# Two more boundaries of a two-block model take the "ahead" form, and the ahead steps are regrouped

## The reference

```python
def modulate(z, g, shift, scale):
    return rmsnorm(z, g) * (1.0 + scale) + shift
def swiglu(h, wi, wo):
    a, u = jnp.split(h @ wi, 2, axis=-1)
    return (jax.nn.silu(a) * u) @ wo
# in each layer, three times with different parts:
x = x + 0.5 * m[2] * swiglu(modulate(x, norm_g[l, 0], m[0], m[1]), ffn1_wi[l], ffn1_wo[l])
```

## Time and profile before

| | us |
|---|---|
| median of three executions | 3223.28 |
| the profiled execution | 3223.28 |
| its span, first to last instruction | 3221.5 |
| matmul engine busy | 3134.3 (97%) |
| VectorE busy | 1885.6 (59%) |
| ScalarE busy | 1035.2 (32%) |

### The profile page before, as it was taken

How to read it: one execution, slowest core, us unless ns; L and a number is a source line. 1 busy time by engine, 2 the same in 40 slices (tenths; PEclk the granted TensorE clock), 3 DMA queues, 4 the chain that set the end, 5 groups by cost and what they waited for, 6 DMA issues and landing times.

```text
span 3221.5 us, 37195 instructions
## 1 busy us (share of the span) xinstructions
PE 3134.3 (97%) x15095; PEld 2518.2 (78%) x15106; DVE 1885.6 (59%) x2713; ACT 1035.2 (32%) x1498; POOL 10.2 (0%) x23
## 2 busy tenths in 40 slices
PE   8999999998899999999999999999999998899998
PEld 6888888776678888788877888788887764578887
DVE  7876555646575554666656554566665555574444
ACT  4212222335542222322234222332224444442222
POOL 0000000000000000000000000000000000000000
PEclk9999999999999999999999999999999999799999
DMA  6433332210034443255522443235552210133231
GB/s 230 140 118 129 146 124 85 65 45 11 1 138 138 149 144 118 91 203 189 204 86 79 175 139 131 79 118 204 188 183 63 72 53 1 53 118 104 93 98 52
DMA packets 102422, 367.13 MB, mean 114 GB/s; under 512 B 11311, under 2 KB 12607, under 8 KB 101997
## 3 DMA queue, kind: packets, MB, share of 16 engines
q1 hardware_dynamic: 101212, 360.04, 32.7%
q0 software_dynamic: 1040, 4.71, 0.4%
HBM read 362.61 MB, written 2.10 MB: 113 GB/s over the span
## 4 chain that ended last, share of the span: by engine, by line
PE 88%; DVE 6%; ACT 3%; issue 1%; DMA 1%; SPq 0%; POOL 0%; DVEq 0%; ACTq 0%; POOLq 0%
PE ps L192 25%; PE ps L194 25%; PE ps L193 25%; PE ps L196 4%; PE ps L197 2%; DVE SQ L614 1%; PE ps L499 1%; DVE HL L603 1%; PE ps L2888 1%; DVE WL L184 1%; PE ps L2858 1%; DVE XT L1037 0%; PE ps L2788 0%; PE ps L2555 0%; DVE RAW L1499 0%
## 5 line engine op out<-in xcount | busy, mean ns | idle before, releaser
L192 PE MATMUL ps<-HH,WH 128*128 128x512 f32 x2432 | 959.5, 395 | 6.9 <-DVE HL L603 3.1
L194 PE MATMUL ps<-HH,WL 128*128 128x512 f32 x2432 | 947.7, 390 | 0.0
L193 PE MATMUL ps<-HL,WH 128*128 128x512 f32 x2432 | 946.9, 389 | 0.0
L179 ACT ACTIVATE WH<-RAW 128x1024 fp32r<-128x1024 f32 x456 | 458.5, 1047 | 622.0 <-PE ps L194 367.2
L184 DVE TENSOR_TENSOR WL<-RAW,WH 128x1024 fp32r<-128x1024 f32 x456 | 542.9, 1220 | 78.0 <-ACT WH L179 77.8
L192 PEld LDWEIGHTS ps<-HH,WH 128*128 128x128 f32 x2432 | 456.5, 188 | 116.1 <-issue 12.2
L194 PEld LDWEIGHTS ps<-HH,WL 128*128 128x128 f32 x2432 | 456.5, 188 | 96.8
L193 PEld LDWEIGHTS ps<-HL,WH 128*128 128x128 f32 x2432 | 456.8, 188 | 95.9 <-issue 4.3
L1037 DVE SCALAR_TENSOR_TENSOR XT<-ps,DER,XT 128x512 f32<-128x512 f32 x512 | 346.6, 683 | 249.9 <-PE ps L194 235.1
L192 PE MATMUL ps<-GH,WH 128*128 128x512 f32 x1056 | 412.9, 391 | 4.8 <-DVE GL L945 4.8
L194 PE MATMUL ps<-GH,WL 128*128 128x512 f32 x1056 | 411.1, 389 | 0.0
(11 more groups left out here) (382 smaller groups left out, 2542.5 us busy)
## 6 DMA issues: line engine op xcount, KB each, us to landing
RAW<-in_w_modt SPq DMA_DIRECT2D x200, 512.0 KB, 5.0
RAW<-in_ffn_wi SPq DMA_DIRECT2D x178, 512.0 KB, 4.9
RAW<-in_w_gu SPq DMA_DIRECT2D x90, 512.0 KB, 4.5
RAW<-in_ffn_wo SPq DMA_DIRECT2D x88, 512.0 KB, 4.9
RAW<-in_w_in SPq DMA_DIRECT2D x44, 512.0 KB, 3.6
RAW<-in_w_down SPq DMA_DIRECT2D x44, 512.0 KB, 4.2
RAW<-in_w_out SPq DMA_DIRECT2D x16, 512.0 KB, 4.5
STG<-in_w_modt SPq DMA_DIRECT2D x10, 512.0 KB, 12.8
```

Source lines behind the costliest of these rows:

```text
L179: act.e.activation(u.hi, u.ld.view, ACT.Copy).then_inc(u.hi_done.sem, 1)
L192: pe.e.matmul(out, wh, x[0], start=first, stop=False)
L193: pe.e.matmul(out, wh, x[1], start=False, stop=False)
L194: m = pe.e.matmul(out, wl, x[0], start=False, stop=last)
```

## The change

* Stages 3 and 5 take the ahead form too: the last down of stage 2 and the pool mixer write UH and UL and full sums of squares; the bias dots for them run in the tails of stages 2 and 3; stages 3 and 5 begin with Factor, NormSplit and chunk 0 on UH and UL. The norm sums, spreads and fillers before these two stages and the filler Busy(4) of the pool mixer go.
* AheadHi and AheadLo become one step, AheadSplit, placed after the product step of d (before, AheadHi stood in front of it), and the last sum of squares, SumsEnd, stands after AheadSplit of block 6 instead of before AheadLo of block 6.
* UpRest goes; its work is part of Up for chunk 0, before the splits of chunk 2.
* Factor's matmul stands after k=2 instead of k=1, and Root after the square of block 6 instead of block 2.
* With the ahead form, the condition spread and the modulation dots of stages 3 and 5 start two chunks later.

```diff
             P.total = self.add[7]
         elif k == 7:
             P.sat = [(P.SA, self.add[5]), (P.SQ[:, 0, :], self.sq[6]), (P.SQ[:, 1, :], self.sq[7])]
-        if k == (2 if self.full else 6):
+        if k == 6:
             self.root = Root(P)
     def square(self, act, k):
...
         act.wait_ge(*self.gain)
         act.e.activation(P.UH[:, k, :], P.XT[:, k, 0:T], ACT.Identity, scale=P.mod_a(self.mi, k)).then_inc(self.hi.sem, 1)
-
-class AheadLo(Step):
-
-
-    def __init__(self, of):
-        self.of = of
-
-    def vector(self, dve):
-        of = self.of
-        P, k = of.P, of.k
-        dve.wait_ge(*of.hi)
-        dve.e.scalar_tensor_tensor(P.UL[:, k, :], P.XT[:, k, 0:T], P.mod_a(of.mi, k), P.UH[:, k, :].bitcast(F32),
-                                   ALU.mult, ALU.subtract).then_inc(of.lo.sem, 1)
+    def vector(self, dve):
+        P, k = self.P, self.k
+        dve.wait_ge(*self.hi)
+        dve.e.scalar_tensor_tensor(P.UL[:, k, :], P.XT[:, k, 0:T], P.mod_a(self.mi, k), P.UH[:, k, :].bitcast(F32),
+                                   ALU.mult, ALU.subtract).then_inc(self.lo.sem, 1)
 class Factor(Step):
...
                 for k in range(8):
                     for q in range(2):
                         products(q, n, k)
-                    if self.factor and k == 1:
+                    if self.factor and k == 2:
                         self.factor.sum(pe)
         else:
             for q in range(2):
...
                 act.wait_ge(*self.done[q, n])
                 if q == 0:
                     act.wait_ge(*self.sfree[n])
+                if q == 0 and self.factor:
+                    act.wait_ge(*self.scaled[q])
+                    act.wait_ge(*self.biased)
+                    act.e.activation(s, s, ACT.Silu, bias=P.BIAS[:, q:q + 1]).then_inc(self.silu[n].sem, 1)
+                    continue
                 if n:
                     if q:
                         act.wait_ge(*self.sxfree)
...
                     dve.wait_ge(*self.factor.done)
                     dve.wait_ge(*self.sfree[n])
                     dve.e.tensor_tensor(d, out, self.factor.R, ALU.mult).then_inc(self.scaled[q].sem, 1)
+                    if q:
+                        dve.wait_ge(*self.silu[n])
+                        dve.wait_ge(*self.scaled[q])
+                        dve.wait_ge(*self.biased)
+                        dve.e.scalar_tensor_tensor(s, d, P.BIAS[:, q:q + 1], s, ALU.add, ALU.mult).then_inc(self.mul[n].sem, 1)
+                        dve.wait_ge(*self.hi[n])
+                        dve.e.tensor_tensor(gl, s, gh.bitcast(F32), ALU.subtract).then_inc(self.lo[n].sem, 1)
                     continue
                 if n:
                     d = F.SX[:, :] if q else s
...
                     dve.e.tensor_tensor(s, s, F.SX[:, :] if n else out, ALU.mult).then_inc(self.mul[n].sem, 1)
                     dve.wait_ge(*self.hi[n])
                     dve.e.tensor_tensor(gl, s, gh.bitcast(F32), ALU.subtract).then_inc(self.lo[n].sem, 1)
-
-
-class UpRest(Step):
-
-
-
-    def __init__(self, up):
-        self.up = up
-
-    def scalar(self, act):
-        up = self.up
-        F, P = up.F, up.P
-        s, gh, gl = up.tiles(0)
-        act.wait_ge(*up.scaled[0])
-        act.wait_ge(*up.biased)
-        act.e.activation(s, s, ACT.Silu, bias=P.BIAS[:, 0:1]).then_inc(up.silu[0].sem, 1)
-        act.wait_ge(*up.mul[0])
-        act.wait_ge(*F.gfree.get(up.c - F.NG, NONE))
-        act.e.activation(gh, s, ACT.Copy).then_inc(up.hi[0].sem, 1)
-
-    def vector(self, dve):
-        up = self.up
-        F, P = up.F, up.P
-        s, gh, gl = up.tiles(0)
-        dve.wait_ge(*up.silu[0])
-        dve.wait_ge(*up.scaled[1])
-        dve.wait_ge(*up.biased)
-        dve.e.scalar_tensor_tensor(s, F.S[:, 1, :], P.BIAS[:, 1:2], s, ALU.add, ALU.mult).then_inc(up.mul[0].sem, 1)
-        dve.wait_ge(*up.hi[0])
-        dve.e.tensor_tensor(gl, s, gh.bitcast(F32), ALU.subtract).then_inc(up.lo[0].sem, 1)
 class Down:
...
                     if dot and fs == tail[0]:
                         bias["lds"] = self.bias_loads(dot[1])
                     for d in range(8):
-                        if nxt is not None and last and d:
-                            hi = self.add(AheadHi(self, nxt, d - 1, down.evac[d - 1, 0][0]))
                         self.add(DownPart(down, d))
                         if nxt is not None and last and d:
-                            if d == 7:
-                                self.add(SumsEnd(sums))
-                            self.add(AheadLo(hi))
+                            self.add(AheadSplit(self, nxt, d - 1, down.evac[d - 1, 0][0]))
                         if d in (1, 3, 5):
                             split_ahead()
                         if dot and fs == tail[0] and d == 5:
...
                         if dot and fs == tail[1] and d in (2, 4):
                             self.add((BiasSum if d == 2 else BiasCopy)(bias["dot"]))
                     if nxt is not None and last:
-                        self.add(AheadLo(self.add(AheadHi(self, nxt, 7, down.evac[7, 0][0]))))
+                        self.add(SumsEnd(sums))
+                        self.add(AheadSplit(self, nxt, 7, down.evac[7, 0][0]))
                 return ([wo[f] for f in fs], run, "in pieces")
             tail, jobs, halves, first = groups[-2:], [], [], 2 if ahead else 0
...
         def job(d):
             def run(units):
-                hi = self.add(AheadHi(self, nxt, d - 1, evac[d - 1])) if d else None
                 out = self.add(OutMM(self, mi, mix, d, units[0], bfree, sums))
                 self.over, evac[d] = out.done, out.evac
-                if d == 7:
-                    self.add(SumsEnd(sums))
                 if d:
-                    self.add(AheadLo(hi))
+                    self.add(AheadSplit(self, nxt, d - 1, evac[d - 1]))
                 if d == 1:
                     bias["lds"] = self.bias_loads(wi)
                 elif d == 2:
...
                 means[g] = self.add(PoolMean(self, copies[g], M, band, ztile, bfree))
             def add(g):
-                return [self.add(PoolAdd(self, mi, means[g], o, bfree, sums)) for o in range(2)][1]
+                for o in range(2):
+                    k = 2 * g + o
+                    adds[k] = self.add(PoolAdd(self, mi, means[g], o, bfree, sums))
+                    if k:
+                        self.add(AheadSplit(self, mi + 1, k - 1, adds[k - 1].evac))
+                return adds[k]
             prod(0)
             prod(1)
...
             copy(3)
             add(2)
             mean(3)
-            self.add(Busy(self, 4))
             last = add(3)
+            self.add(SumsEnd(sums))
+            self.add(AheadSplit(self, mi + 1, 7, last.evac))
         return [last.evac]
     def mixer_ab(self, mi, after, following):
...
                             0, (3, 4, 5, 6, 7, 8), (2,))
         over = self.mixer_ab(1, over, first(a["ffn2_wi"][0]))
         over = self.ffn(2, X, a["ffn2_wi"][0], a["ffn2_wo"][0], over, first(a["ffn1_wi"][1]), 1, (0, 1, 2),
-                        ahead=True)
-        over = self.ffn(3, X, a["ffn1_wi"][1], a["ffn1_wo"][1], over, None, 1, (3, 4, 5, 6, 7, 8))
+                        ahead=True, nxt=3, dot=(3, a["ffn1_wi"][1]))
+        over = self.ffn(3, X, a["ffn1_wi"][1], a["ffn1_wo"][1], over, None, 1, (3, 4, 5, 6, 7, 8),
+                        ahead=True, dot=(5, a["ffn2_wi"][1]))
         over = self.mixer_pool(4, over, first(a["ffn2_wi"][1]))
-        over = self.ffn(5, X, a["ffn2_wi"][1], a["ffn2_wo"][1], over, first(a["w_gu1_2"]), 2, (0, 1, 2))
+        over = self.ffn(5, X, a["ffn2_wi"][1], a["ffn2_wo"][1], over, first(a["w_gu1_2"]), 2, (0, 1, 2), ahead=True)
         self.final_norm("final_g", True)
         over = self.ffn(6, X, a["w_gu1_2"], a["w_down1_2"], over, [a["w_in_2"][DQ], a["w_in_2"][DV]],
                         2, (3, 4, 5, 6, 7, 8))
```

More of the change, by code:

```diff
@@ L665, in vector @@
         self.sums.late(dve, 8)
-class AheadHi(Step):
+class AheadSplit(Step):
     def __init__(self, P, mi, k, ready):
@@ L897, in scalar @@
         F, P, c = self.F, self.P, self.c
-        if self.factor:
-            return
         for q in range(2):
@@ L3247, in ffn @@
                 self.add(NormSplit(self, mi, segs, F.h, after, R=R))
-                leading = self.add(Up(F, 0, units))
+                self.add(Up(F, 0, units))
             else:
@@ L3255, in up @@
             def up(c):
-                def run(units):
-                    if ahead and c == 1:
-                        self.add(UpRest(leading))
-                    self.add(Up(F, c, units))
-                return ([wi[c], wi[NF + c]], run)
+                return ([wi[c], wi[NF + c]], lambda units: self.add(Up(F, c, units)))
             def down(fs):
@@ L3381, in run @@
                 elif d == 7:
-                    self.add(AheadLo(self.add(AheadHi(self, nxt, 7, evac[7]))))
+                    self.add(SumsEnd(sums))
```

(5 more changed lines are left out.)

## The result

The changed kernel took 3252.2 us in the median (3252.1 to 3254.9, four executions) against 3222.3 beside it: ratio 1.0089 [1.0070, 1.0107], 29.9 us slower. Forecast were 3250 us and 27.2 us. In a later set of runs the ratio was 1.0089 [1.0075, 1.0103] again, 30.0 us.

What follows compares the result with a forecast made beforehand. The matmul engine, busy 97% of the span, was taken as the bound. 4.25 + 4.0 + 1.6 + 5.5 + 4.5 + 0.9 = 20.75 us, with the clock 27.2, on 3223.3 gave 3250 us; 8-in-10 range 3238 to 3260.

Steps and rivals of the forecast that it cites:

- part 1: Stages 2 and 8: UpRest's work, ahead of chunk 2's weight halves, makes chunk 2 start 4.25 and 4.0 us later.
- part 2: Out projections: UL waits for UH behind the square, so the wait behind BiasDot grows 0.8 us, twice: 1.6 us.
- part 3: Last down of stage 2: the 2.75 us chain per block exceeds 2.04 us of matmuls; stage 3's chunk 2 5.5 us later.
- Falls at the two sum waits cost nothing: Factor matmul waits of stages 3 and 5: clock falls there cost 0, since VectorE sets chunk 2's start.
- part 4: Pool mixer: the same 2.75 us chain per block makes chunk 2 of stage 5 start 4.5 us later.
- part 5: Small items: two BiasSum pairs on the matmul engine cost 0.9 us; BiasDot, extra loads and later dots cost 0.
- part 6: Granted clock: falls to 1.2 GHz behind the waits before chunk 2 in stages 2, 3, 5 and 8, 6.4 us.
- I count a fall at each of the four: Chunk 2 of stages 2, 3, 5 and 8: a clock fall behind each wait, 1.6 us lost each time.
- B: Rival, chance 0.18: the waits before chunk 2 come but the clock stays up there; 3244 us.
- C: Rival, chance 0.09: the sum at the Factor matmul of stages 3 and 5 does not wait; 3231 us, 3238 with clock.
- F: Rival, chance 0.02: the table load before chunk 2 costs twice its row, 1.3 us more at four boundaries; 3255 us.
- D: Rival, chance 0.04: VectorE and ScalarE keep up everywhere, stages 3 and 5 gain 7.8 and 9.0 us; faster, 3207 us.

Runs made afterwards that it cites:

- a_rest: Changed kernel with UpRest put back as a step of its own after the splits of chunk 2: 3229.4 us, ratio 1.0009 to the kernel before.
- b_merge: Kernel before with only UpRest merged into Up for chunk 0 (stages 2 and 8): 3237.9 us, ratio 1.0032.
- e_table: Changed kernel with a one-column Silu added in each ahead stage to load its table earlier: 3245.3 us, ratio 1.0058 to the kernel before.
- d_order: Changed kernel with the ahead steps back in the order of before in all four places: 3238.9 us, ratio 1.0035 to the kernel before.
- after again: The changed kernel itself, run and traced a second time with no edit: 3253.4 us, ratio 1.0089 to the kernel before.
- before again: Kernel before with Root moved from block 2 to block 6 in the full sums of the two out projections: 3224.9 us, ratio 0.9998.

## Why the prediction was right, step by step

1. **UpRest (part 1, 4.25 and 4.0)**: X+27.92 and X+27.13 in the trace, 4.33 and 4.20 us later than before. Shown by a_rest and b_merge; 1.28 us of it is the load (e_table).
2. **UH behind the square (part 2, 1.6)**: waits of 2.61 for 1.81, twice; d_order takes them back.
3. **Last down of stage 2 (part 3, 5.5)**: chunk 2 came 50.45 us after evac(0), 50.5 were forecast. Inside, the wait at the Factor matmul was 5.82 (6.2) and the wait at chunk 2 2.59 (5.3): chunk 0 ran its next products at 0.50 clock, which used up 2.7 us of the later wait. "Falls at the two sum waits cost nothing" held.
4. **Pool mixer (part 4, 4.5)**: from the mark in front of it (the last down of stage 3) chunk 2 comes at 85.98 us, before it would have been 81.26: 4.7. The inner numbers were off and made up for each other: chunk 0 starts 4.7 later, not 2.8, as the means wait for evac (1.29) as well as for Z (3.68, where it was 1.61 in the earlier trace rows), and so the Factor matmul waits 2.61, not 5.4.
5. **Small (part 5, 0.9)**: 0.45 was put in each of two stretches, and about 0.1 is left in each: stage 3 is 5.6 us longer, 5.5 of it chunk 2; stage 5 is 6.4 longer, 4.7 of it chunk 2 and 1.6 clock.
6. **Clock (part 6, 4 x 1.6)**: right in sum, by chance in its parts. The third chunk, once begun, takes 2.8, 0, 1.6 and 1.7 us longer in stages 2, 3, 5 and 8 (6.1). The step that failed is "I count a fall at each of the four": in stage 3 the wait had shrunk to 2.59 and no fall came, and the fall of stage 2 cost more than 1.6.
7. **What no part has**: the first stretch, +5.95 in the first pair of traces with 0.8 forecast. That is scatter of the unchanged mixer (910.8 to 918.1 over thirteen traces). The span difference of that pair, 31.8, is therefore partly luck. Against the second trace of before it is 26.2, with a first stretch 1.3 us shorter; in the one pair with equal first stretches (918.12, after again and before again) the spans differ by 27.7. The medians say 29.9 and 30.0. Some 3 us between medians and sum stay open.

Of the signs that the prediction named, the waits behind BiasDot, those at chunk 2 of stages 2 and 8 and the one at the Factor matmul of stage 3 came as written. Four did not: no window at 0.50 behind the wait at chunk 2 of stage 3, 2.59 and 3.67 us at chunk 2 of stages 3 and 5, where 4 to 5 were named, and 2.61 us at the Factor matmul of stage 5, where 5 to 6 were named. The start of chunk 2 was right there all the same, since VectorE sets it whatever the matmul engine has waited before; so the mechanism held, and the forecast of how the waits are shared did not.

Rivals: B (clock stays) and C (the sum does not wait) are out by the rows above. F is out by e_table. D is out for this change; without the regrouping, the ahead form does make the kernel faster, by 10.7 us.

## What to carry over

An operation that costs nothing where it stands may be covered by its place in the queue alone: before moving it in front of something that another engine waits for, count it and all its hand-overs in full. Where two in-order engines pass a block back and forth, place each step so that the one waiting on the other has other work in between; then count the whole work of the fuller engine, the planner's weight splits too. Compare stretches between fixed marks, and take a second trace of the kernel before, since unchanged code may move by as much as the change.

## What the hardware showed that I had not expected

The clock falls behind waits of equal length in one run and not in another. Behind BiasDot in mixer ab, after 1.80 us, it fell in two traces of eight; after 2.60 us in four of five; in the hybrid, after the same waits, in none of thirteen. In front of chunk 2 it fell behind all twelve waits from 3.65 to 5.10 us, behind the one of 3.42, behind 3.55 in one of two, and behind none of 2.76 or less. A fall cost 1.5 to 2.8 us. The Trainium skill (TensorE: Matmul & The Clock Gate, Part 1: The HAM clock gate) says that the chip looks at activity in a rhythm of its own that does not start with the kernel; scatter at equal waits is what that would give, and mixer ab agrees (6 falls in 13). It does not say why none of thirteen came in the hybrid mixer, and no run here shows it.

A fall in front of a second wait was free here: the 1.2 GHz stretch behind the Factor matmul of stage 3 cost 2.7 us and shortened the wait at chunk 2 by as much, and behind that shorter wait the clock stayed up.
